# Attention stage of a streaming encoder step: logits of odd items issued behind the projection parts, softmax weights of the two narrow tiles scaled by VectorE

## The chip, the cores and the metric

One core of a Trainium2 chip runs the whole program. The time is device microseconds (us) of one execution, and the comparison is of medians over several executions of the two kernels.

## What is computed

One layer over 640 tokens (512 of a prompt, 8 samples with 16 new frames each), width 1024, in fp32. Every product of two large matrices is made of three matmuls over split operands (a high and a low half of each), so that fp32 accuracy is kept.

```python
x = x + 0.5 * swiglu(rmsnorm(x, ffn1_norm), ffn1_w_gate, ffn1_w_up, ffn1_w_down)
h = rmsnorm(x, mix_norm)
z = h @ w_in                        # gates, conv inputs, q, k, v, index queries and keys
...
conv_out = gb * conv                # 3-tap causal conv of gc * xv
score = einsum(relu(index dots), wi); top n_sel keys of each token
logits = einsum(q, k_sel) * HEAD_DIM ** -0.5
p = softmax(logits); o = einsum(p, v_sel)
x = x + concat([conv_out, attn]) @ w_out
x = x + 0.5 * swiglu(rmsnorm(x, ffn2_norm), ffn2_w_gate, ffn2_w_up, ffn2_w_down)
```

## The kernel before

The program has three stages: the first feed-forward block (to about 450 us), the mixer (450 to about 720 us) and the second feed-forward block. The change is nearly all in the last part of the mixer, the **attention items** (585 to 712 us).

**Items.** There are 40 items, `ITEMS[n]` for n = 0 to 39: five tiles of tokens in the order 3, samples, 2, 1, 0 (`ATT_TILES`, the samples are tile 4), and eight items (heads, or samples) in each. A tile's keys are 512, 384, 384, 256 and 128 columns wide. So items 16 to 23 are tile 2 (384 columns), items 24 to 31 tile 1 (256) and items 32 to 39 tile 0 (128); tiles 1 and 0 are the narrow ones. One item passes through these steps:

- TensorE writes the logits into PSUM bank 4 or 5 (`logits_pair`, two heads at once, L937; `logits_sample`, L921 to L926). It waits until the bank's last logits have been read.
- VectorE adds the mask, stores the sum into one of four weight slots and takes the row's minimum (`masked_min`, L2115, which frees the bank); for the samples it takes a minimum alone (L2109).
- ScalarE takes the exponential in place and its row sum (`exp_out`, L1418, or L1414 for the samples).
- The row is divided by its sum: on ScalarE for items 0 to 7, on VectorE for items 8 to 11 (`normalise`, L2126 and L2127), on GpSimd from item 12 (`GPSIMD_FROM`, L2353 and L2354).
- TensorE transposes the weights into bank 6 (`turn_weights`, L854), once per item in tiles 3, 4 and 2, once for two items in tile 1, once for four in tile 0. ScalarE copies the bank out (`weights_out`, L1102 `hid<-ps`), and TensorE multiplies by the values (`weigh_sample_values`, L965; `weigh_four_heads`, L979).

**Parts.** Between these, TensorE works off 64 *parts* (`filler`), each six matmuls of 320 columns (L596, L598, L600): 32 of the conv projection, then 32 of the output projection. `parts_by(n)` says how many are done by the end of item n; items 8, 12, 20, 28 and 36 have none. Parts left over follow item 39. When a block of parts is complete, VectorE evicts it (`proj_out`, L2077 for the output projection). Part 32 and its three followers need the conv output, split by ScalarE and VectorE (`conv_hi`, `conv_lo`, in items 8 to 11 by `CONV_SPLITS`).

**What sets the order.** It is written out by hand. Each engine runs its own loop over n. `issued_by(n)` gives how far the logits, the masked minima and the exponentials have been issued by item n: n + 3 up to item 14, 19 in item 15, n + 5 from item 16 on. A pair of logits is issued when its even item comes up, so from item 16 on in even items, behind `turn_weights` and ahead of the parts. VectorE's loop further holds the last rounds of the top-k selection (`top_rounds`, L2062 and L2063; the mask of tile 1 is finished in item 19, by `ROUNDS`), the low halves of the next weights in quarters (`quarter_lo_of`, L1557, by `QUARTERS`) or whole (`mixer_lo`, L1548), and the low half of a finished tile's output (`attended_lo`, L2134). ScalarE makes the high halves.

**In the feed-forward blocks** four hidden blocks are made in the plain way and the rest in pairs of sets inside a loop. `plain_hid(3)` (L1647, L1651), the last step of the fourth plain block, stands on VectorE behind the loop and ahead of the last pair (`period(PAIRS - 1, ...)`). Its result is first read by ScalarE's `rest_hi(1)`, behind the last pair.

## Time and profile before

| | before |
|---|---|
| median of three executions | 1164.75 us (1164.25 to 1165.76) |
| profiled execution, its time | 1166.49 us |
| profiled execution, its span | 1164.60 us |
| TensorE busy | 1154.6 us (99%) |
| VectorE busy | 916.1 us (79%) |
| ScalarE busy | 526.1 us (45%) |
| GpSimd busy | 94.7 us (8%) |

The span is what the profiler saw from the first to the last instruction, and 1.9 us lie around it. TensorE's busy share hides two things: matmuls run longer when a lower clock is granted and are still busy, and the page's slices of 29 us don't show waits of a few us. So the attention items have to be read in a timeline.

### The profile page before, as it was taken

What the parts mean: (1) busy time and instruction counts of PE and PEld (TensorE: products, weight loads), DVE (VectorE), ACT (ScalarE), POOL (GpSimd) and SP (SyncE); (2) the same over time, 40 slices, a digit from 0 to 9 for tenths busy, and PEclk for the clock granted to TensorE, in tenths of its full rate; (3) what the DMA queues carried; (4) which work ended last, traced back from release to release, by engine and by line L of the source; (5) the groups of instructions that cost most, each with busy time, mean ns of one, the idle gap of its engine ahead of it and who ended that gap; (6) DMA issues with size and microseconds to landing.
All of it is one profiled execution on the core that took longest, in us unless ns stands there. A gap on an engine that the chain in (4) does not pass through costs nothing.

```text
span 1164.6 us, 20299 instructions
## 1 busy us (share of the span) xinstructions
PE 1154.6 (99%) x7704; PEld 1107.3 (95%) x7704; DVE 916.1 (79%) x1402; ACT 526.1 (45%) x791; POOL 94.7 (8%) x130
## 2 busy tenths in 40 slices
PE   9999999999999999999999899999999999999999
PEld 9999999999999999867987679999999999999998
DVE  6998777877989982467998753798877778798996
ACT  6354444444445552361234452434444444454452
POOL 0000000000000000102473351000000000000000
PEclk9999999999999999999999899999999999999999
DMA  7212221222332233201321023321322222124222
GB/s 249 85 55 91 86 95 72 98 82 67 124 146 80 73 109 119 73 37 37 145 73 37 1 67 107 129 73 37 109 72 84 96 72 98 64 100 154 103 87 84
DMA packets 22992, 103.98 MB, mean 89 GB/s; under 512 B 3344, under 2 KB 6288, under 8 KB 13584
## 3 DMA queue, kind: packets, MB, share of 16 engines
q1 hardware_dynamic: 21792, 99.67, 24.2%
q10 hardware_dynamic: 1136, 3.43, 1.0%
q8 instruction: 43, 0.70, 0.3%
q14 instruction: 21, 0.17, 0.0%
HBM read 96.99 MB, written 6.10 MB: 89 GB/s over the span
## 4 chain that ended last, share of the span: by engine, by line
PE 91%; DVE 7%; issue 1%; ACT 1%; DVEq 0%; POOL 0%; ACTq 0%; POOLq 0%
PE ps L656 18%; PE ps L658 18%; PE ps L657 18%; PE ps L596 8%; PE ps L600 8%; PE ps L598 8%; PE ps L587 2%; PE ps L589 2%; PE ps L588 2%; DVE score L2063 1%; PE ps L854 1%; DVE top L2062 1%; DVE wl L1548 1%; PE ps L937 1%; PE ps L863 1%
## 5 line engine op out<-in xcount | busy, mean ns | idle before, releaser
L1102 ACT ACTIVATE wh<-raw 128x1024 fp32r<-128x1024 f32 (+4 forms) x206 | 202.4, 985 | 261.6 <-PE ps L658 142.9
L656 PE MATMUL ps<-xs,wh 128*128 128x320 f32 x976 | 300.2, 308 | 0.5 <-ACT snap L1102 0.5
L657 PE MATMUL ps<-xs,wh 128*128 128x320 f32 x976 | 300.2, 308 | 0.0
L658 PE MATMUL ps<-xs,wl 128*128 128x320 f32 x976 | 300.1, 308 | 0.0
L656 PEld LDWEIGHTS ps<-xs,wh 128*128 128x128 f32 x976 | 182.9, 187 | 1.0 <-issue 1.0
L658 PEld LDWEIGHTS ps<-xs,wl 128*128 128x128 f32 x976 | 182.9, 187 | 0.0
L657 PEld LDWEIGHTS ps<-xs,wh 128*128 128x128 f32 x976 | 182.9, 187 | 0.0
L596 PE MATMUL ps<-xh,wh 128*128 128x320 f32 x544 | 131.1, 322 | 0.0
L1672 DVE TENSOR_TENSOR wl<-raw,wh 128x1024 fp32r<-128x1024 f32 (+1 forms) x108 | 112.7, 1044 | 19.4 <-ACT wh L1102 18.3
L600 PE MATMUL ps<-xh,wl 128*128 128x320 f32 x544 | 124.7, 311 | 0.0
L598 PE MATMUL ps<-xl,wh 128*128 128x320 f32 x544 | 124.6, 311 | 0.0
L1102 ACT ACTIVATE snap<-ps 128x320 f32<-128x320 f32 x156 | 68.0, 437 | 121.1 <-PE ps L658 120.6
L596 PEld LDWEIGHTS ps<-xh,wh 128*128 128x128 f32 x544 | 90.0, 189 | 12.6 <-issue 11.1
L598 PEld LDWEIGHTS ps<-xl,wh 128*128 128x128 f32 x544 | 91.8, 189 | 0.0
L600 PEld LDWEIGHTS ps<-xh,wl 128*128 128x128 f32 x544 | 91.7, 189 | 0.0
L658 PE MATMUL ps<-xr,wl 128*128 128x320 f32 x288 | 88.9, 309 | 0.0
L656 PE MATMUL ps<-xr,wh 128*128 128x320 f32 x288 | 88.9, 309 | 0.0
L657 PE MATMUL ps<-xr,wh 128*128 128x320 f32 x288 | 88.9, 309 | 0.0
L1672 DVE TENSOR_TENSOR wl<-sums,wh 128x1024 fp32r<-128x1024 f32 x36 | 44.1, 1225 | 38.1 <-ACT wh L1102 38.1
L1102 ACT ACTIVATE wh<-sums 128x1024 fp32r<-128x1024 f32 x52 | 54.8, 1053 | 24.0 <-DVE sums L1687 14.4
L1548 DVE TENSOR_TENSOR wl<-raw,wh 128x2048 fp32r<-128x2048 f32 (+2 forms) x31 | 56.5, 1823 | 11.5 <-ACT wh L1102 11.5
L1783 DVE TENSOR_TENSOR wl<-raw,wh 128x1024 fp32r<-128x1024 f32 (+1 forms) x48 | 49.9, 1041 | 6.1 <-ACT wh L1102 6.1
(282 smaller groups left out, 2134.4 us busy)
## 6 DMA issues: line engine op xcount, KB each, us to landing
raw<-gu SPq DMA_DIRECT2D x42, 1024.0 KB, 4.8
raw<-dn SPq DMA_DIRECT2D x16, 1024.0 KB, 5.3
raw<-dn SPq DMA_DIRECT2D x12, 512.0 KB, 3.8
raw<-wconv SPq DMA_DIRECT2D x6, 1024.0 KB, 4.9
raw<-wout SPq DMA_DIRECT2D x4, 1024.0 KB, 4.8
x<-xt SPq DMA_DIRECT2D x12, 320.0 KB, 4.7
raw<-wtok SPq DMA_DIRECT2D x4, 840.0 KB, 4.3
x_keep<-x SPq DMA_DIRECT2D x8, 320.0 KB, 2.2
```

Source lines behind the costliest of these rows:

```text
L587: pe.matmul(out, ah, bh, start=first, stop=False)
L588: pe.matmul(out, ah, bl, start=False, stop=False)
L596: pe.matmul(o, ah, bh[:, c], start=first, stop=False)
L598: pe.matmul(o, ah, bl[:, c], start=False, stop=False)
L600: last_mm = pe.matmul(o, al, bh[:, c], start=False, stop=last)
L656: pe.matmul(out, ah, bh, start=first, stop=False, skip_group_check=True)
L657: pe.matmul(out, ah, bl, start=False, stop=False, skip_group_check=True)
L658: return pe.matmul(out, al, bh, start=False, stop=last, skip_group_check=True)
L1102: return nc.scalar.activation(out, in_, ACT.Copy, scale=scale)
L1548: dve.tensor_tensor(wl[:, slot, 0:n], raw[:, slot, 0:n], wh[:, slot, 0:n].bitcast(F32), ALU.subtract).then_inc(lo_ready, 1)
L1672: dve.tensor_tensor(ring(wl_flat, part), set_source(slot, part), ring(wh_flat, part).bitcast(F32), ALU.subtract)\
L1783: dve.tensor_tensor(ring(wl_flat, part), set_source(slot, part), ring(wh_flat, part).bitcast(F32), ALU.subtract)\
```

## The change

1. **Order of the logits.** `issued_by(n)` is n + 4 from item 15 on. The pairs of logits are then issued in odd items (18 and 19 in item 15, 20 and 21 in item 17, and so on), and behind the parts instead of ahead of them. On VectorE the masked minima from item 15 on stand at the end of an item, behind the top rounds, evictions and quarters; ScalarE's exponentials follow the same `issued_by`.
2. **Parts one item earlier.** Item 8 has a part, and four parts instead of five are left after item 39. `CONV_SPLITS` moves to items 7 to 10 and waits for `chunks_used` (the first four chunks of the last conv block have been read) instead of for all conv projections.
3. **The first unit of output weights in quarters.** The high and low halves of `U_OUT` are made in four quarters in items 4 to 7, not whole in item 3. The third unit's quarters move from items 27, 28, 29 and 33 to 26, 27, 28 and 32. In item 15 ScalarE makes its quarter ahead of the exponentials.
4. **Scaling of the narrow tiles.** Items 24 to 39 are divided by their sums on VectorE (`VECTOR_FROM` = 24), the weights of item n + 2 in item n, and no longer on GpSimd.
5. **Feed-forward blocks.** `plain_hid(3)` moves on VectorE into the last half period of the last pair, and ScalarE waits for it ahead of `rest_hi(1)`.

```diff
@@ parts_by, tables, issued_by @@
-            return 32 + n - 8 - sum(m <= n for m in WITHOUT_PART)
+            return 32 + n - 7 - sum(m <= n for m in WITHOUT_PART)
...
-        PROJ_SPLITS = {0: U_CONV + 5, item_of(9): U_OUT}
-        QUARTERS = {14 + q: (U_OUT + 1, q) for q in range(4)}
+        PROJ_SPLITS = {0: U_CONV + 5}
+        QUARTERS = {4 + q: (U_OUT, q) for q in range(4)}
+        QUARTERS |= {14 + q: (U_OUT + 1, q) for q in range(4)}
...
-        GPSIMD_FROM = 12
+        GPSIMD_FROM, VECTOR_FROM = 12, 24
...
-            return min(n + 3 if n < 15 else 19 if n == 15 else n + 5, len(ITEMS))
+            return min(n + 3 if n < 15 else n + 4, len(ITEMS))
...
-        CONV_SPLITS = {8: (0,), 9: (1,), 10: (2,), 11: (3,)}
+        CONV_SPLITS = {7: (0,), 8: (1,), 9: (2,), 10: (3,)}
@@ TensorE, loop over the items @@
-                for ahead in range(issued_by(n - 1), issued_by(n)):
-                    logits(ahead)
+                if n < 15:
+                    for ahead in range(issued_by(n - 1), issued_by(n)):
+                        logits(ahead)
                 for i in range(parts_by(n - 1), parts_by(n)):
                     filler(i)
+                if n >= 15:
+                    for ahead in range(issued_by(n - 1), issued_by(n)):
+                        logits(ahead)
@@ ScalarE @@
+                act.wait_ge(hid_ready, PLAIN * (k + 1))
                 for n in (1, 2):
                     rest_hi(n)
...
                 if n in CONV_SPLITS:
-                    act.wait_ge(proj_job, NPROJ)
+                    act.wait_ge(chunks_used, 1)
...
-                if n in QUARTERS and ITEMS[n][0] != 4:
+                if n in QUARTERS and (ITEMS[n][0] != 4 or n == 15):
                     quarter_hi_of(*QUARTERS[n])
@@ VectorE, feed-forward @@
+                    if not ahead:
+                        plain_hid(3)
                     out_of(p, slot, 0, block)
...
-                plain_hid(3)
                 period(PAIRS - 1, 0, pair_block(PAIRS - 1))
@@ VectorE, normalise and the loop over the items @@
-                wait_bank_read(dve, job)
+                if t == 4:
+                    wait_bank_read(dve, job)
+                else:
+                    dve.wait_ge(exp_ready, nth_of_kind(n) + 1)
...
+                if VECTOR_FROM <= n + 2 < len(ITEMS):
+                    normalise(n + 2)
+                if n < 15:
+                    for ahead in range(issued_by(n - 1), issued_by(n)):
+                        masked_min(ahead)
...
                 if n in (25, 33):
                     attended_lo(n // 8 - 1)
+                if n >= 15:
+                    for ahead in range(issued_by(n - 1), issued_by(n)):
+                        masked_min(ahead)
@@ GpSimd @@
-            for n in range(GPSIMD_FROM, len(ITEMS)):
+            for n in range(GPSIMD_FROM, VECTOR_FROM):
                 normalise(n)
```

TensorE in item 15 before, from its transposes to those of item 16 (`tab` holds the identity of the transposes, `kt,q_all` are logits, `xh`, `xl` with `wh`, `wl` a part, `hid` with `ikc_v`, `zkv` the product with the values):

```order
L854 MATMUL ps<-tab,score 128x128 x3
L937 MATMUL ps<-kt,q_all 128x384 x2
L596 MATMUL ps<-xh,wh 128x320 x2
L598 MATMUL ps<-xl,wh 128x320 x2
L600 MATMUL ps<-xh,wl 128x320 x2
L965 MATMUL ps<-hid,ikc_v 64x64 x2
L965 MATMUL ps<-hid,zkv 64x64
L965 MATMUL ps<-hid,ikc_v 64x64 x2
L965 MATMUL ps<-hid,zkv 64x64
L854 MATMUL ps<-tab,rp 128x128 x3
```

The same place after:

```order
L857 MATMUL ps<-tab,score 128x128 x3
L599 MATMUL ps<-xh,wh 128x320 x2
L601 MATMUL ps<-xl,wh 128x320 x2
L603 MATMUL ps<-xh,wl 128x320 x2
L942 MATMUL ps<-kt,q_all 128x384 x2
L973 MATMUL ps<-hid,ikc_v 64x64 x2
L973 MATMUL ps<-hid,zkv 64x64
L973 MATMUL ps<-hid,ikc_v 64x64 x2
L973 MATMUL ps<-hid,zkv 64x64
L857 MATMUL ps<-tab,rp 128x128 x3
```

The part now stands ahead of the logits of items 18 and 19, and item 16 (from the last row on) has no logits of its own.

VectorE before, from the masked minimum of item 16 (first row) to that of item 18 (last row). `MAX` and `MATCH_REPLACE` are a top round of tile 1, `wl<-raw,wh` is a quarter:

```order
L2115 ISA rp,stat<-ps,mask 128x384
L2115 ISA stat 128x1
L2062 MAX top<-score 128x8
L2063 MATCH_REPLACE score<-top,score 128x256
L1557 TENSOR_TENSOR wl<-raw,wh 128x512
L2115 ISA rp,stat<-ps,mask 128x384
L2115 ISA stat 128x1
L2115 ISA hid,stat<-ps,mask 128x384
```

The same place after:

```order
L2129 ISA rp,stat<-ps,mask 128x384
L2129 ISA stat 128x1
L2076 MAX top<-score 128x8
L2077 MATCH_REPLACE score<-top,score 128x256
L1570 TENSOR_TENSOR wl<-raw,wh 128x512
L2076 MAX top<-score 128x8
L2077 MATCH_REPLACE score<-top,score 128x256
L1570 TENSOR_TENSOR wl<-raw,wh 128x512
L2129 ISA rp,stat<-ps,mask 128x384
L2129 ISA stat 128x1
L2129 ISA hid,stat<-ps,mask 128x384
L2129 ISA stat 128x1
```

A second top round and a second quarter now stand ahead of the masked minimum of item 17.

VectorE in tile 1 before, from the masked minimum of item 26 on:

```order
L2115 ISA rp,stat<-ps,mask 128x256
L2115 ISA stat 128x1
L2077 SCALAR_TENSOR_TENSOR x<-ps,x 128x640
L2115 ISA rp,stat<-ps,mask 128x256
L2115 ISA stat 128x1
L2115 ISA hid,stat<-ps,mask 128x256
L2115 ISA stat 128x1
L2115 ISA hid,stat<-ps,mask 128x256
```

VectorE in tile 1 after, from the masked minimum of item 24 on:

```order
L2129 ISA rp,stat<-ps,mask 128x256
L2129 ISA stat 128x1
L2143 RECIPROCAL stat<-stat 128x1
L2144 TENSOR_SCALAR rp<-rp,stat 128x256
L2129 ISA rp,stat<-ps,mask 128x256
L2129 ISA stat 128x1
L2143 RECIPROCAL stat<-stat 128x1
L2144 TENSOR_SCALAR rp<-rp,stat 128x256
```

Each masked minimum is now followed by the reciprocal and the multiply of the same item, and only then by the next masked minimum.

## Rows read from the trace of the kernel before

**Rows 1.** waits of TensorE: us in total, times, longest

```profile
PE ps L937 <- DVE stat L2115: 4.0, 3, 2.4
...
PE ps L656 <- ACT snap L1102: 0.5, 2, 0.2
...
PE ps L965 <- ACT hid L1102: 0.4, 1, 0.4
...
PE ps L854 <- DVE rp L2127: 0.3, 1, 0.3
```

**Rows 2.** windows: length, busy PE, PEld, DVE, ACT, POOL, PEclk, DMA share, GB/s

```profile
640.00:657.00 17.00, 17.00 (x165) 12.26 (x160) 14.53 (x37) 7.71 (x20) 5.48 (x8) 1.00 0.00 1
...
660.00:680.00 20.00, 18.82 (x94) 13.30 (x94) 11.99 (x37) 10.10 (x26) 9.14 (x15) 0.68 0.25 83
```

**Rows 3.** timeline of PE: start, us, engine, line, operation, [idle before <-releaser]

```profile
656.97 0.55 PE L854 MATMUL ps<-tab,score 128*128 128x128 f32 x3
...
659.91 1.65 PE L937 MATMUL ps<-kt,q_all 64*128 64x384 f32 x4 [2.39 <-DVE stat L2115]
...
666.53 1.65 PE L937 MATMUL ps<-kt,q_all 64*128 64x384 f32 x4 [1.14 <-DVE stat L2115]
...
669.88 0.84 PE L854 MATMUL ps<-tab,rp 128*128 128x128 f32 x3
...
672.12 0.84 PE L854 MATMUL ps<-tab,hid 128*128 128x128 f32 x3
...
674.72 0.49 PE L854 MATMUL ps<-tab,score 128*128 128x128 f32 x3
...
676.02 1.51 PE L979 MATMUL ps<-hid,zkv 128*64 128x256 f32 x12
...
680.27 0.52 PE L854 MATMUL ps<-tab,hid 128*128 128x128 f32 x3 [0.18 <-ACT hid L1102]
...
705.53 0.60 PE L854 MATMUL ps<-tab,rp 128*128 128x128 f32 x4
```

**Rows 4.** timeline of DVE, 650 to 666 us

```profile
650.26 0.56 DVE L2109 TENSOR_REDUCE stat<-ps 128x1 f32<-128x384 f32 x1 [0.56 <-PE ps L926]
...
655.93 0.82 DVE L2077 SCALAR_TENSOR_TENSOR x<-ps,x 128x640 f32<-128x640 f32 x1
...
656.67 0.55 DVE L2115 CUSTOM_DVE_ANT_0 rp<-ps,mask 128x384 f32<-128x384 f32 x1
...
658.59 0.69 DVE L1557 TENSOR_TENSOR wl<-raw,wh 128x512 fp32r<-128x512 f32 x1 [0.51 <-ACT wh L1102]
...
659.20 0.55 DVE L2115 CUSTOM_DVE_ANT_0 rp<-ps,mask 128x384 f32<-128x384 f32 x1
...
665.23 0.69 DVE L2134 TENSOR_TENSOR xl<-ps,xh 128x512 fp32r<-128x512 f32 x1 [1.04 <-ACT xh L1102]
```

**Rows 5.** timeline of DVE and of ACT: one narrow item's operations

```profile
638.27 0.15 DVE L2126 RECIPROCAL stat<-stat 128x1 f32<-128x1 f32 x1
...
638.45 0.42 DVE L2127 TENSOR_SCALAR rp<-rp,stat 128x384 f32<-128x384 f32 x1
...
678.68 0.42 DVE L2115 CUSTOM_DVE_ANT_0 rp<-ps,mask 128x256 f32<-128x256 f32 x1 [1.54 <-PE ps L937]
...
678.05 0.49 ACT L1102 ACTIVATE hid<-ps 128x384 f32<-128x384 f32 x1 [1.36 <-PE ps L854]
...
679.15 0.51 ACT L1418 ACTIVATE rp<-rp,stat 128x256 f32<-128x256 f32 x1 [0.60 <-DVE stat L2115]
...
679.57 0.19 ACT L1418 ACTIVATION_READ_ACCUMULATOR rp<-rp,stat 128x1 f32 x1
...
698.76 0.40 ACT L1418 ACTIVATE rp<-rp,stat 128x128 f32<-128x128 f32 x1 [1.67 <-DVE stat L2115]
```

**Rows 6.** timeline, end of the first feed-forward loop: DVE, then PE

```profile
265.93 0.82 DVE L1647 SCALAR_TENSOR_TENSOR hid<-sq_pair,hid 128x640 f32<-128x640 f32 x1
...
270.86 0.39 PE L656 MATMUL ps<-xs,wh 128*128 128x320 f32 x1 [0.25 <-ACT snap L1102]
```

More of the change, by code:

```diff
@@ L230, in trunk @@
         proj_job = sem("proj_job")
+        chunks_used = sem("chunks_used")
         proj_evac = sem("proj_evac")
@@ L260, in trunk @@
         p_ready = sem("p_ready")
+        p_narrow_ready = sem("p_narrow_ready")
         p_sample_ready = sem("p_sample_ready")
@@ L350, in quarters_before @@
         def quarters_before(U):
-            return 3 * (0 if U == U_CONV else U - U_OUT)
+            return 3 * (0 if U == U_CONV else 1 + U - U_OUT)
         def first_part(buf, i):
@@ L894, in proj_part @@
                     pe.wait_ge(lo_ready, U + 1)
-                    if U in (U_CONV, U_OUT + 1, U_OUT + 2):
+                    if U in (U_CONV, U_OUT, U_OUT + 1, U_OUT + 2):
                         pe.wait_ge(quarter_lo, quarters_before(U) + 3)
@@ L909, in proj_part @@
                     mm.then_inc(proj_job, 1)
+                if b == NPROJ - 1 and c == 3:
+                    mm.then_inc(chunks_used, 1)
             def proj(b):
@@ L949, in turn_weights @@
             def turn_weights(n):
-                pe.wait_ge(p_sample_ready if ITEMS[n][0] == 4 else p_ready, nth_of_kind(n) + 1)
+                if n >= VECTOR_FROM:
+                    pe.wait_ge(p_narrow_ready, n - VECTOR_FROM + 1)
+                else:
+                    pe.wait_ge(p_sample_ready if ITEMS[n][0] == 4 else p_ready, nth_of_kind(n) + 1)
                 first = n if n < 24 else n - 1 if n < 32 else n - 3
@@ L1525, in _ @@
                     exp_out(ahead)
-                if n in QUARTERS and ITEMS[n][0] == 4:
+                if n in QUARTERS and ITEMS[n][0] == 4 and n != 15:
                     quarter_hi_of(*QUARTERS[n])
@@ L2124, in normalise @@
                 job = ("logit", n)
-                wait_bank_read(dve, job)
+                if t == 4:
+                    wait_bank_read(dve, job)
+                else:
+                    dve.wait_ge(exp_ready, nth_of_kind(n) + 1)
                 link(dve.reciprocal(stat[:, 80 + n:81 + n], stat[:, 40 + n:41 + n]))
                 dve.tensor_scalar(weights(n)[:, 0:width[t]], weights(n)[:, 0:width[t]], stat[:, 80 + n:81 + n],
-                                  None, ALU.mult).then_inc(p_sample_ready, 1)
+                                  None, ALU.mult).then_inc(p_sample_ready if t == 4 else p_narrow_ready, 1)
             def attended_lo(i):
@@ L2250, in _ @@
                     normalise(n + 1)
-                for ahead in range(issued_by(n - 1), issued_by(n)):
-                    masked_min(ahead)
+                if VECTOR_FROM <= n + 2 < len(ITEMS):
[3 more added lines that the diff above has]
+                        masked_min(ahead)
                 for t, rounds in ROUNDS.items():
```

## The prediction

> **What bounds the kernel now.** I read the list of TensorE's waits first, then the windows over the attention items, then TensorE's timeline there and VectorE's beside it. TensorE is the bound: it is busy 99% of the span, so work on other engines counts only where it makes TensorE wait, or where it keeps TensorE at its lower clock. The list shows about 7 us of waits in all; 4.0 of them are logits that wait for VectorE's masked minimum [rows 1]. Two of the three lie in items 15 and 16: 2.39 us ahead of the logits of items 18 and 19, and 1.14 us ahead of those of 20 and 21 [rows 3]. What the list doesn't show is the clock. In the window from 660 to 680 us the mean granted clock is 0.68, in that from 640 to 657 us it is 1.00 [rows 2]. 0.68 means 12.8 us at 1.2 GHz and the rest at 2.4 GHz, and the fall comes with the 2.39 us wait. At the low clock, transposes and a part take 2.24 us (669.88 to 672.12), at the full one 1.30 (674.72 to 676.02) [rows 3], a factor of about 1.75. Of the 12.8 us, 1.1 are waiting, so 11.7 x (1 - 1/1.75) = 5.0 us are lost to the clock. The attention items thus lose 2.39 + 1.14 + 5.0 = 8.5 us around items 15 to 18, and 0.8 elsewhere (0.4, 0.3 and 0.18 [rows 1, 3]). Everything behind 720 us is TensorE without a wait, so what the items gain or lose passes to the end.
>
> The wait of 2.39 us is VectorE running behind. It last waits for TensorE at 650.26 us (samples' logits of item 14) and then has no pause up to the masked minimum of item 16 at 656.67; that of item 17 follows at 659.20 and releases TensorE 0.71 us later [rows 3, 4].
>
> **Feed-forward part of the change.** `plain_hid(3)` takes 1.6 us on VectorE just ahead of the last pair, and TensorE waits 0.25 us for a snapshot there [rows 6]; the list has it twice, 0.5 us in all, once per block [rows 1]. In its new place VectorE has no set to sum for a next pair, which is what hides it. The new wait on ScalarE holds `rest_hi(1)`, and behind it the operands of the rest units, until a step that was done some 10 us before. I take the 0.5 us as gained; if the cover were missing, 1.6 us on VectorE would come back as at most 0.5 us here. **-0.5 us.**
>
> **Items 0 to 14.** The first unit's halves are made in quarters in items where TensorE doesn't wait, instead of whole; the sum of the work is the same. The transfer that follows into the freed buffer starts four items later and is needed only from item 26. Parts come one item earlier: item 8 has one, and it hides the two waits of items 8 and 9 (0.4 and 0.3 us, for ScalarE's copy and VectorE's scaling [rows 1]). A part is 1.0 of the 1.30 us that transposes and a part take [rows 3]; this one is saved behind item 39, where parts follow each other and take 0.9. `chunks_used` lets the conv halves start before the last projection is complete. If a half came late instead, item 8's part would wait, by something like those 0.7 us. So item 15 starts at 656.97 + 1.0 - 0.7 = 657.3 us [rows 3].
>
> **Items 15 to 21.** Here the new order is decided. VectorE's waiting point of item 12 shifts with TensorE by 0.3 to 650.6; the masked minimum of item 16 came 6.41 us behind it, of which 0.74 are an eviction (655.93 to 656.67) that now lies in item 11 [rows 4]: 656.3. Before, the minimum of item 17 followed 2.53 us behind (a top round, a quarter, 0.5 us of waiting for ScalarE). Now one more top round (658.59 - 656.67, less 0.51 of waiting and 0.47 for the minimum = 0.94) and one more quarter (658.59 to 659.20 = 0.61) stand ahead of it: 656.3 + 2.53 + 0.94 + 0.61 = 660.4, and TensorE is released 0.71 later, at 661.1 [rows 4]. TensorE has its transposes and the part behind it at 657.3 + 1.3 = 658.6 to 658.7. **The part no longer comes behind the wait but ahead of it, and the wait is as long as it was, 2.4 us**, since VectorE's share in front of it grew by 1.55 us.
>
> The clock will then most likely fall again. The first stretch without any wait brought it back before (from 669.88 [rows 3]), and now TensorE has work from 661.1 for 5 to 7 us (logits, product, and the parts of items 16 and 17). I take 3 us of loss; the ends are 0 and some 6.
>
> The next pair (20, 21) waits for the minimum of item 19. Its row of VectorE work: the minimum of 18 at 662.7 (logits at the low clock take 1.65 us [rows 3]), `attended_lo` (with 1.0 us of waiting for ScalarE before it, as at 665.23 [rows 4]), a top round, an eviction, a quarter, the minimum: 668.1. TensorE is there at about 667.8, waits some 0.4 us, and issues at 668.3. Then the minimum of item 20 (0.94 + 0.61 + 0.55 after 668.1) and its exponential hold ScalarE's copy of the transposes of item 18, and item 19's transposes start at 671.4, 1.0 us late. Item 19 is 1.3 us for transposes and part, 0.85 for logits and 1.45 for the product with the values [rows 3], so item 20 starts at 675.0. Now the transposes of 20 and 21 stand back to back, where a pair of logits lay between; the second needs the bank copied out (0.55 [rows 3] + 0.49 [rows 5] and 0.1 of signals = 1.15 instead of 0.5). With 2.0 us for item 21, **item 22 starts at 678.0** against 680.27 before, and one part more is done by then. At full clock all through it would be 677.2, with a long low stretch 679.5.
>
> **Items 22 to 39.** GpSimd's 16 scalings hid behind everything; on VectorE they form a chain. VectorE's queue is now minimum n, reciprocal and multiply n, minimum n + 1, and the multiply needs the exponential of the same item. The rows for 256 columns [rows 5]: 0.47 from the minimum to the exponential (678.68 to 679.15), 0.61 until the row sum is read, 0.03, 0.18 from reciprocal to multiply, and 0.27 for the multiply (0.33 of step at 384 columns, taken down for the width): 1.56 us. For 128 columns the same steps are 0.34 + 0.50 (0.40 and the sum's read-out [rows 5]) + 0.03 + 0.18 + 0.20 = 1.25, an estimate where no row has the width. That is 8 x 1.56 + 8 x 1.25 = 22.5 us, in which nothing else fits, because the queue is in order. To it come four quarters (2.5), three evictions (2.2) and two `attended_lo` (0.6 of 0.69 each): 28.4 us [rows 4]. The chain starts 0.2 us behind item 22's start, waits about 1.3 us for TensorE (logits 26, eviction 15) and 0.6 for ScalarE's quarters and signals. So the transposes that end it, item 39's, start 30.7 us behind item 22. Before, they came 705.53 - 680.27 = 25.3 us behind [rows 3]. **+5.4 us**, in waits of 0.5 to 1.5 us ahead of the logits of 30, 32, 34, 38 and the product of 27 and 31. The low end, without the two additions, is 28.9 (+3.6); the high end 32.
>
> GpSimd, which loses this work, has nobody waiting for it: `norm_factors(2)`, behind it in its queue, comes later. Scaling would cost nothing if the cover were still there; it is the order of the queue that costs.
>
> **The sum,** by marks of the timeline: item 39's transposes at 678.0 + 30.7 = 708.7 against 705.5 (+3.2); one part less behind them (-0.9); the feed-forward waits (-0.5). That is **+1.8 us**: a span of 1166.4 us, 1168.3 for a profiled execution with the 1.9 us around it. The median shown is 1.7 us under the profiled execution before, so the median comes to 1164.75 + 1.8 = **1166.5 us**.
>
> **Rivals.** (a) *The clock falls again in the narrow tiles* or stays low for longer than I take in items 15 to 19. For it: the chain leaves TensorE idle in short pieces, and two (1.2 us each) are 4 us apart in items 27 to 29. Against it: 0.6 us of waits at 637 to 639 us brought no fall. The price is 1 to 4 us on the forecast, 1168 to 1170.5, since TensorE has slack to the chain for part of it. The Trainium skill (TensorE: Matmul & The Clock Gate, "A second HAM failure mode: psum-queue depth-cycling") tells of a kernel whose clock swung because TensorE was idle for moments between groups of matmuls. By that page this rival would be the rule; no row here shows such a fall. It decides if the median is above 1168. (b) *The chain doesn't bind.* If exponentials are ready before VectorE comes to the multiply, the narrow tiles keep their 25.3 us: 1166.5 - 5.4 = 1161.1. It would take VectorE two minima ahead, and the queue shows that it can't be. (c) *No second fall* at item 15, since the transposes are now followed by a part: item 22 at 677.2 and the chain at its low end, 0.8 + 1.8 us better: 1164. (d) *The reordering does nothing*: waits only change places, 1164.75.
>
> **Chances.** The forecast (1165.5 to 1168) 0.42, (a) 0.24, (b) or anything beyond 2.3 us of gain 0.14, (c) and (d) 0.20. A change of 0.2% (2.3 us) is about what a measurement of this kernel can tell from none. The forecast itself lies within it, and a quarter of it and most of (a) beyond: faster 0.15, same 0.48, slower 0.37. Range 1162.8 to 1170.0.
>
> **What would show it.** Right: a wait of about 2.4 us ahead of the logits of items 18 and 19, behind a part; a granted clock below 1 around 660 us, for less than 12.8 us; item 22's transposes near 678; VectorE in tile 1 with a wait for ScalarE ahead of each reciprocal, 1.5 us from minimum to minimum, and TensorE waits summing to 4 to 6 us between items 22 and 39; no snapshot wait at 271 us. Wrong: no wait at item 15 (then my VectorE count from 650 us is off), or TensorE without waits in the narrow tiles (then the chain is hidden).

## The result and the profile after

The changed kernel takes 1169.63 us (median of six executions, 1169.39 to 1171.06), the kernel before 1165.2 us in the same session (1164.25 to 1166.27). The ratio is 1.0044, 95% interval 1.0033 to 1.0055: by the medians 4.4 us **slower**. The profiled execution took 1171.06 us with a span of 1169.1 us, 4.5 us over the span before.

TensorE's waits after (us in total, times, longest):

```profile
PE ps L942 <- DVE stat L2129: 7.5, 7, 2.3
PE ps L857 <- ACT hid L1114: 2.9, 4, 1.7
PE ps L987 <- ACT hid L1114: 1.4, 3, 0.5
...
PE ps L857 <- DVE rp L2144: 0.8, 1, 0.8
```

The waits for the masked minimum (L2129; the logits are at L942) grew from 4.0 us in three to 7.5 us in seven [rows 1]. Waits for ScalarE's copies of the transposed weights (`hid`) come to 4.3 us, where they were 0.6. The two waits for a snapshot [rows 1] are gone. The timeline of TensorE at the marks of [rows 3], which are the transposes of items 15, 19, 22 and 39 and the logits of (18, 19) and (20, 21):

```profile
658.79 0.55 PE L857 MATMUL ps<-tab,score 128*128 128x128 f32 x3
...
662.51 1.65 PE L942 MATMUL ps<-kt,q_all 64*128 64x384 f32 x4 [2.30 <-DVE stat L2129]
...
669.59 0.92 PE L942 MATMUL ps<-kt,q_all 64*128 64x384 f32 x4 [1.41 <-DVE stat L2129]
...
673.78 0.52 PE L857 MATMUL ps<-tab,score 128*128 128x128 f32 x3 [1.67 <-ACT hid L1114]
...
680.59 0.55 PE L857 MATMUL ps<-tab,hid 128*128 128x128 f32 x3
...
711.42 0.66 PE L857 MATMUL ps<-tab,rp 128*128 128x128 f32 x4
```

Item 15 starts 1.8 us later than before (one part more is done by then), item 22 0.3 later, item 39 5.9 later. The span is 4.5 us longer, so behind item 39 the changed kernel is 1.4 us faster. Two windows, with the granted clock in the third column from the right:

```profile
656.00:664.00 8.00, 5.70 (x38) 3.52 (x36) 5.66 (x17) 3.32 (x8) 3.65 (x6) 0.91 0.00 0
...
690.00:712.00 22.00, 17.28 (x121) 13.68 (x120) 13.28 (x55) 10.87 (x33) 0.00 (x0) 1.00 0.13 49
```

The clock falls again at the wait of 2.30 us, and for less time: the mean from 660 to 680 us is 0.91, where it was 0.68 [rows 2]. By the same working as in the prediction that is 3.6 us at 1.2 GHz and 1.5 us lost, 3.5 less than before. In the narrow tiles TensorE is idle for 4.7 of 22 us, in short pieces, and the clock stays at 2.4 GHz. The balance of the two profiles: all waits of TensorE sum to 15.0 us instead of 7.2, 7.8 more, and 3.5 us less are lost to the clock; that makes 4.3 of the 4.5 us.

### The profile page after: what moved, and what is told of

It is laid out like the page before. It is cut to its first block, busy times and chain, and to the rows that moved or that the text cites. A ratio compares the mean times of both kernels' runs of the same rounds, so it can differ in the third digit from the quotient of the medians.

```text
span 1169.1 us, 20306 instructions
## 1 busy us (share of the span) xinstructions
PE 1151.4 (98%) x7704; PEld 1104.6 (94%) x7704; DVE 925.8 (79%) x1437; ACT 526.1 (45%) x794; POOL 78.7 (7%) x98
## 4 chain that ended last, share of the span: by engine, by line
PE 86%; DVE 10%; issue 2%; ACT 2%; DMA 1%; ACTq 0%; DVEq 0%
PE ps L659 18%; PE ps L660 18%; PE ps L661 18%; PE ps L599 7%; PE ps L603 7%; PE ps L601 7%; PE ps L590 2%; PE ps L592 2%; PE ps L591 2%; DVE score L2077 2%; DVE top L2076 2%; DVE wl L1561 1%; PE ps L866 1%; PE ps L857 1%; DMA raw<-gu 1%
```

## The experiments

Each kernel was timed beside the kernel before. In the table, "15 to 22" is the time from the transposes of item 15 to those of item 22 in the profiled execution, "22 to 39" the same for the items behind; both are differences of two starts in TensorE's timeline, as above. The kernel before has medians of 1164.10 to 1165.2 us in the different sessions, so kernels of two sessions are compared here by what each is above or below the kernel before. A star marks a stretch in which that execution had a low clock for some microseconds.

| kernel | median us | before, same session | ratio (95%) | 15 to 22 | 22 to 39 |
|---|---|---|---|---|---|
| before | 1165.2 | | | 23.30* | 25.26 |
| after | 1169.63 | 1165.2 | 1.0044 (1.0033 to 1.0055) | 21.80* | 30.83 |
| e1 after, scaling on GpSimd | 1169.15 | 1164.57 | 1.0041 (1.0028 to 1.0055) | 22.87* | 29.76 |
| e2 after, scaling behind the minimum | 1168.36 | 1164.57 | 1.0040 (1.0026 to 1.0054) | 21.51* | 29.66 |
| e3 before, scaling on VectorE | 1164.89 | 1164.57 | 1.0004 (0.9995 to 1.0013) | 19.83 | 25.92 |
| e4 before, part 5 | 1163.42 | 1164.57 | 0.9990 (0.9981 to 0.9999) | 19.84 | 25.25 |
| e5 before, part 1 | 1168.84 | 1164.10 | 1.0035 (1.0021 to 1.0048) | 21.15* | 29.12 |
| e6 e1, minimum of 17 earlier | 1168.10 | 1164.10 | 1.0031 (1.0021 to 1.0042) | 19.94 | 29.76 |
| e7 after, minimum of 17 earlier | 1169.17 | 1164.10 | 1.0035 (1.0022 to 1.0049) | 20.89* | 30.82 |
| e8 before, parts 2 and 3 | 1163.28 | 1164.10 | 0.9990 (0.9981 to 0.9999) | 20.66* | 25.44 |
| e9 e1, quarters behind the minimum | 1164.30 | 1164.22 | 1.0002 (0.9993 to 1.0012) | 18.87 | 27.68 |
| e10 after, quarters behind the minimum | 1164.61 | 1164.22 | 1.0003 (0.9994 to 1.0012) | 18.88 | 28.07 |
| e11 after, quarters and scaling behind it | 1163.84 | 1164.22 | 0.9997 (0.9988 to 1.0006) | 18.87 | 27.49 |
| e12 before, parts 2, 3, 5, minimum of 17 in item 14 | 1160.36 | 1164.22 | 0.9967 (0.9954 to 0.9979) | 17.41 | 25.45 |
| e13 e11, logits ahead of the parts | 1169.81 | 1164.16 | 1.0053 (1.0039 to 1.0066) | 21.69* | 30.47 |
| e14 before, minimum of 17 in item 14 | 1161.42 | 1164.16 | 0.9976 (0.9967 to 0.9985) | 18.21 | 25.26 |
| e15 before, parts 2, 3, 5 | 1162.66 | 1164.16 | 0.9984 (0.9975 to 0.9993) | 19.89* | 25.43 |
| e16 e12, scaling of item 9 first | 1160.19 | 1164.16 | 0.9966 (0.9954 to 0.9978) | 17.67* | 25.43 |

### Is it the scaling? (e1 to e3)

The forecast had put 5.4 us on the scaling of the narrow tiles, so that was undone first.

```diff
-        GPSIMD_FROM, VECTOR_FROM = 12, 24
+        GPSIMD_FROM, VECTOR_FROM = 12, 40
```

> The changed kernel with part 4 alone undone: all weights from item 12 on are divided on GpSimd again. Theory A (the scaling on VectorE costs the time): items 22 to 39 took 25.3 us before and 30.8 after, so about 5.5 us go: 1164.1 us, 1.1 us faster than before, TensorE waits of about 5 us in items 22 to 39 gone. Rival B (the logits behind the parts are what costs there, whoever scales): less than 2 us go, 1168 us or more. Rival C (half each): 1166 to 1167.

Theory A fell: the kernel is still 4.6 us above the kernel before, where the changed one is 4.4, and items 22 to 39 still take 29.76 us. In them 1.1 us came back, not 5.5. Rival B had the number right. VectorE's timeline shows why. After, from the masked minimum of item 28 (first row) to that of item 30:

```profile
689.64 0.41 DVE L2129 CUSTOM_DVE_ANT_0 hid<-ps,mask 128x256 f32<-128x256 f32 x1
689.98 0.08 DVE L2129 DVE_READ_ACCUMULATOR2_ANT stat<- 128x1 f32 x1
690.73 0.16 DVE L2143 RECIPROCAL stat<-stat 128x1 f32<-128x1 f32 x1 [0.67 <-ACT hid L1431]
690.93 0.35 DVE L2144 TENSOR_SCALAR hid<-hid,stat 128x256 f32<-128x256 f32 x1
691.25 0.69 DVE L1570 TENSOR_TENSOR wl<-raw,wh 128x512 fp32r<-128x512 f32 x1
691.86 0.42 DVE L2129 CUSTOM_DVE_ANT_0 hid<-ps,mask 128x256 f32<-128x256 f32 x1
...
693.96 0.69 DVE L1570 TENSOR_TENSOR wl<-raw,wh 128x512 fp32r<-128x512 f32 x1 [0.45 <-ACT wh L1114]
694.56 0.42 DVE L2129 CUSTOM_DVE_ANT_0 score<-ps,mask 128x256 f32<-128x256 f32 x1
```

The same place in e1, VectorE and then ScalarE:

```profile
689.24 0.41 DVE L2129 CUSTOM_DVE_ANT_0 hid<-ps,mask 128x256 f32<-128x256 f32 x1
...
690.85 0.69 DVE L1570 TENSOR_TENSOR wl<-raw,wh 128x512 fp32r<-128x512 f32 x1 [1.19 <-ACT wh L1114]
691.46 0.42 DVE L2129 CUSTOM_DVE_ANT_0 hid<-ps,mask 128x256 f32<-128x256 f32 x1
...
693.56 0.71 DVE L1570 TENSOR_TENSOR wl<-raw,wh 128x512 fp32r<-128x512 f32 x1 [1.67 <-ACT wh L1114]
694.19 0.41 DVE L2129 CUSTOM_DVE_ANT_0 score<-ps,mask 128x256 f32<-128x256 f32 x1
```

```profile
689.70 0.51 ACT L1431 ACTIVATE hid<-hid,stat 128x256 f32<-128x256 f32 x1 [1.59 <-DVE stat L2129]
690.12 0.18 ACT L1431 ACTIVATION_READ_ACCUMULATOR hid<-hid,stat 128x1 f32 x1
690.21 0.61 ACT L1114 ACTIVATE wh<-raw 128x512 fp32r<-128x512 f32 x1
691.92 0.51 ACT L1431 ACTIVATE hid<-hid,stat 128x256 f32<-128x256 f32 x1 [1.10 <-DVE stat L2129]
```

With and without the scaling it is 2.22 us from the first minimum to the second, and 2.70 or 2.73 to the third. In e1 VectorE stands for 1.19 and 1.67 us ahead of each quarter (`wl<-raw,wh`), for ScalarE's quarter (`wh<-raw`); that one stands in ScalarE's queue behind the exponential, the exponential waits for the minimum, and the next minimum stands on VectorE behind the quarter. That is a **second loop between the two queues**: minimum 0.46 us, exponential with its sum 0.5, ScalarE's quarter 0.6, VectorE's quarter 0.6. In the changed kernel the scaling lies in VectorE's waits within that loop, and one turn of 2.22 us is one item. The kernel before has the same chain, but with the minimum of item n + 4 at the start of item n, ahead of that item's quarter, a turn leads to the next minimum but one. So it spans two items, which take 3.0 us of TensorE's time on average (25.26 us for 17 items), and the turn does not hold them up.

> The changed kernel with one line moved: on VectorE the scaling of item n + 2 stands behind the masked minimum of item n + 3 instead of ahead of it. The same operations on the same engine. Theory A1 (the cost is the serial chain minimum, exponential, reciprocal, multiply of one item, 1.56 us at 256 columns): VectorE no longer stands for 0.67 us ahead of each reciprocal, items 22 to 39 take 26 us or less, 1164.5 to 1165.5 us. Rival A2 (the cost is VectorE's load, 16 x 0.6 us more, in whatever order): 3 us or more of the 5.5 stay, 1167.5 us or more.

The edit moves `normalise(n + 2)` behind `masked_min(n + 3)`. Theory A1 fell: VectorE no longer waits ahead of each reciprocal, and items 22 to 39 take 29.66 us all the same. Rival A2 had the number (1168.36 us), but not the cause, as e3 and e11 show. The median is 0.8 us lower than e1's in the same session; the ratios, 1.0040 and 1.0041, don't tell the two apart. The loop through the quarters is untouched: 2.22 and 2.71 us from minimum to minimum at the same place.

> The kernel before with part 4 alone: items 24 to 39 divided on VectorE, item n + 2 in item n. There the masked minimum of item n + 3 already stands between the minimum and the scaling of item n + 2. Theory A1 (chain): the chain never forms, within 0.7 us of before, 1165 to 1166 us. Rival A2 (load): 3 to 5.5 us slower, 1168 to 1171 us.

```diff
+                if VECTOR_FROM <= n + 2 < len(ITEMS):
+                    normalise(n + 2)
                 for ahead in range(issued_by(n - 1), issued_by(n)):
                     masked_min(ahead)
```

The cut shows the line that matters; the semaphore and the limits of the two loops are as in the diff of the change. Part 4 alone, in the order before, costs nothing that can be measured (1.0004), and 0.66 us in the profile's items 22 to 39. VectorE's load is not the cause.

### Which part loses the time (e4, e5, e8)

> The kernel before with part 5 alone: plain_hid(3) inside the last half period of the last pair. Theory: the two snapshot waits of 0.25 us go, 0.5 us faster, 1164.7 us. Rival (its 1.6 us on VectorE come back at the end of the pair or in the rest units): 1165.2 us or more.

The edit is the two places of `plain_hid(3)` in the diff of the change. Part 5 alone gives 1.1 us by the medians, at the edge of what can be told from nothing (0.1 to 2.2 us by the interval), where 0.5 was expected. The two snapshot waits are gone from its trace, and the timelines show some more: TensorE is 0.74 us behind the kernel before at 25 us and 0.31 behind it at 416 us, a gain of 0.43 in the first block, and behind item 39's transposes the span is 458.63 us instead of 459.07, 0.44 in the second. That is 0.9 us for waits that the list gives as 0.5; the rest of each is not explained.

> The kernel before with part 1 alone: logits pairs in odd items behind the parts, masked minima from item 15 on at the end of an item, and ScalarE's quarter of item 15 ahead of its exponentials (without which that order locks up). The scaling stays on GpSimd. Theory B (the place of the masked minima costs: a second chain through the quarters, minimum, exponential, ScalarE's quarter, VectorE's quarter, minimum, 2.2 us for each item with a quarter): nearly all of the change's loss is here, 1168 to 1170 us, items 22 to 39 in 29 to 30 us. Rival A (the scaling is the cause, and its undoing was hidden by something else): within 1.5 us of before, 1164.5 to 1166.5 us.

```diff
-            return min(n + 3 if n < 15 else 19 if n == 15 else n + 5, len(ITEMS))
+            return min(n + 3 if n < 15 else n + 4, len(ITEMS))
@@ VectorE @@
-                for ahead in range(issued_by(n - 1), issued_by(n)):
-                    masked_min(ahead)
+                if n < 15:
+                    for ahead in range(issued_by(n - 1), issued_by(n)):
+                        masked_min(ahead)
...
+                if n >= 15:
+                    for ahead in range(issued_by(n - 1), issued_by(n)):
+                        masked_min(ahead)
```

The cut leaves out TensorE's logits behind the parts and ScalarE's quarter of item 15, which are as in the diff of the change. Part 1 alone is 4.7 us slower by the medians: the whole loss. Items 22 to 39 take 29.12 us with all the scaling on GpSimd. Theory B holds.

> The kernel before with parts 2 and 3 alone: parts one item earlier, the conv halves in items 7 to 10, the first unit of output weights in quarters in items 4 to 7. Theory: a part more stands ahead of item 9, the two waits of items 8 and 9 (0.61 us) go but 0.8 us return ahead of item 9's transposes, and one part less follows item 39: about 0.3 us slower, 1164.8 to 1165.5 us. Rival (the quarters and the slow conv halves cost nothing by themselves, the 0.8 us come with the rest of the change): 0.6 us faster, 1164 us.

The edit is all of the diff on parts, tables, `CONV_SPLITS` and `chunks_used`. Parts 2 and 3 alone are 0.8 us **faster**, against my expectation and near the rival's 0.6, although the wait of 0.80 us ahead of item 9 is there (639.96 in its timeline). TensorE then comes later to the wait ahead of the logits of 18 and 19, which shrinks from 2.39 to 1.59 us.

### Taking the loops apart (e6, e7, e9 to e11)

> The changed kernel with the scaling on GpSimd again and, on VectorE, from item 15 on the masked minimum of item n + 2 at the start of item n, ahead of top rounds, evictions, attended_lo and quarters (TensorE's order stays that of the change). Theory B: both chains are gone; no wait ahead of the logits of 18 and 19, items 22 to 39 in 25 to 26 us: 1160 to 1163 us, faster than before. Rival D (TensorE's own order, logits behind the parts and transposes back to back, is what costs): 1165 us or more. If the clock at 660 us stays full without that wait, the wait is what brings the fall; if it falls all the same, it is not.

```diff
+                if n >= 15 and n + 2 < len(ITEMS):
+                    masked_min(n + 2)
                 if n == 16 or n == 8:
                     attended_lo(n // 8 - 1)
...
-                if n >= 15:
-                    for ahead in range(issued_by(n - 1), issued_by(n)):
-                        masked_min(ahead)
```

Theory B's number fell, and rival D's (1165 us or more) came out. But the expectation rested on a misreading of my own edit. The start of item n + 1 is the same place in the queue as the end of item n, so only the minimum of item 17 really moved; the loop through the quarters stayed (29.76 us, as in e1). What the run does show: the wait ahead of the logits of 18 and 19 fell from 2.31 to 0.72 us, and 0.73 us ahead of item 17 and 0.79 more ahead of the next pair took nearly all of it back.

> As the kernel with the minima first and GpSimd's scaling, but with the scaling on VectorE as in the change, so that the minimum of item n + 2 and the scaling of item n + 2 stand side by side: the chain of the scaling alone, without the one through the quarters. Theory (two chains of nearly the same length, each of which holds the time alone): items 22 to 39 take 29.5 to 31 us again, 4 to 5 us more than with GpSimd, 1165 to 1167 us. Rival (the scaling never cost anything, in any order): within 1 us of the kernel with GpSimd.

The same edit on the changed kernel, with the same misreading in it: the loop through the quarters is still there, so this is no test of the scaling's chain alone. Items 22 to 39 take 1.1 us more than in e6, and in after 1.1 us more than in e1. So the scaling adds 1.1 us there to a loop that is there already. The medians are 1.1 us apart, too, but the intervals of e6 and e7 overlap nearly whole.

> The changed kernel with the scaling on GpSimd and, on VectorE from item 15 on, the quarter of an item behind its masked minimum instead of ahead of it. Neither chain is left. Theory (two chains, either of which holds items 22 to 39 at 29 to 31 us; the trace of the kernel with the scaling back on GpSimd shows 2.2 to 2.7 us from minimum to minimum wherever a quarter stands between): items 22 to 39 in 25.3 to 26.5 us, 1163.5 to 1165.5 us. Rival D (TensorE's order itself: logits behind the part, transposes back to back): items 22 to 39 stay above 28 us, 1167 us or more.

```diff
-                if n in QUARTERS:
+                if n in QUARTERS and n < 15:
                     quarter_lo_of(*QUARTERS[n])
                 if n in (25, 33):
                     attended_lo(n // 8 - 1)
                 if n >= 15:
                     for ahead in range(issued_by(n - 1), issued_by(n)):
                         masked_min(ahead)
+                if n in QUARTERS and n >= 15:
+                    quarter_lo_of(*QUARTERS[n])
```

With the quarter moved behind the minimum, and nothing else against e1, the time falls from 4.6 us above the kernel before to 0.1 above it, 4.5 us. VectorE's timeline of e9 at the place shown for e1:

```profile
685.48 0.41 DVE L2129 CUSTOM_DVE_ANT_0 hid<-ps,mask 128x256 f32<-128x256 f32 x1
...
685.82 0.42 DVE L2129 CUSTOM_DVE_ANT_0 hid<-ps,mask 128x256 f32<-128x256 f32 x1
...
687.09 0.69 DVE L1570 TENSOR_TENSOR wl<-raw,wh 128x512 fp32r<-128x512 f32 x1 [0.84 <-ACT wh L1114]
687.79 0.42 DVE L2129 CUSTOM_DVE_ANT_0 score<-ps,mask 128x256 f32<-128x256 f32 x1
```

The second minimum now follows 0.34 us behind the first instead of 2.22, the third 2.31 behind the first instead of 4.95. Items 15 to 22 also gain (18.87 us): there, too, a quarter stood ahead of each minimum. The 22.87 us of e1 hold a low clock; e6, with the quarter still ahead and the full clock, takes 19.94. All eleven executions of e9 have a mean clock of 1.000, those of e1 0.997 to 1.000, so a part of the 4.5 us is the clock. Items 22 to 39 take 27.68 us, 2.1 less than in e1 but 2.4 more than before; my 25.3 to 26.5 was too low.

> The changed kernel with only the quarters moved behind the minima; the scaling stays on VectorE ahead of the minimum. The chain of the scaling alone. Theory: items 22 to 39 in 29.5 to 31 us, 3.5 to 5 us more than in the same kernel with GpSimd's scaling, 1167 to 1169.5 us. Rival (the scaling is hidden once the quarters are out of the way): within 1 us of that kernel.

The scaling chain alone costs 0.4 us in items 22 to 39 and 0.3 us in the medians against e9: the theory of two loops of the same length fell. The scaling's chain is there, with 1.55 to 1.60 us from minimum to minimum in items 28 to 31, but TensorE takes 1.5 us for an item anyway, so it holds up little. The trace of e10 shows the quarters filling the chain's gaps; no wait stands ahead of this reciprocal, where after has 0.67 us:

```profile
687.88 0.69 DVE L1570 TENSOR_TENSOR wl<-raw,wh 128x512 fp32r<-128x512 f32 x1
688.63 0.16 DVE L2143 RECIPROCAL stat<-stat 128x1 f32<-128x1 f32 x1
688.83 0.35 DVE L2144 TENSOR_SCALAR hid<-hid,stat 128x256 f32<-128x256 f32 x1
```

> The changed kernel with quarters and scaling both behind the minimum: on VectorE minimum of n + 3, scaling of n + 2, quarter. No chain, all the scaling still on VectorE. Theory: as with GpSimd's scaling to within 0.7 us, 1163.5 to 1166 us. Rival A2 (VectorE's load of 16 x 0.6 us counts in any order): 2 us or more above the kernel with GpSimd's scaling and quarters behind.

As expected: 1163.84 us with all the scaling on VectorE, within 0.5 us of e9. Two moved lines in VectorE's loop take the changed kernel back to the median of the kernel before. They don't undo all that part 1 costs: parts 2, 3 and 5 without it are 1.5 us faster than before (e15), this kernel 0.4, and its items 22 to 39 take 27.49 us instead of 25.26.

### What else TensorE's order does (e13)

> The changed kernel with quarters and scaling behind the minimum on VectorE, and on TensorE the pairs of logits of odd items ahead of the parts again instead of behind them. That kernel without the last edit took 27.5 us for items 22 to 39, 2.2 us more than before, in short waits for ScalarE's copies of the transposes. Theory (the 2.2 us come from the place behind the parts): items 22 to 39 in 25.5 to 26.5 us, 1 to 2 us faster, 1162 to 1163 us. Rival (they come from issuing pairs in odd items at all, where ScalarE's copy of the last transposes is not covered): within 0.5 us of 1163.8 us, or slower by what TensorE then waits for the minimum, up to 1166 us.

```diff
-                if n < 15:
-                    for ahead in range(issued_by(n - 1), issued_by(n)):
-                        logits(ahead)
+                for ahead in range(issued_by(n - 1), issued_by(n)):
+                    logits(ahead)
                 for i in range(parts_by(n - 1), parts_by(n)):
                     filler(i)
-                if n >= 15:
-                    for ahead in range(issued_by(n - 1), issued_by(n)):
-                        logits(ahead)
```

Both expectations failed by far: it is 6.0 us slower than e11. TensorE's waits in e13:

```profile
PE ps L942 <- DVE stat L2125: 7.0, 6, 2.6
PE ps L857 <- DVE rp L2140: 2.2, 2, 1.4
PE ps L857 <- ACT hid L1110: 1.8, 2, 1.1
```

The logits then wait for a minimum that comes at an item's end, and the part that could have run meanwhile stands behind them. So the placing behind the parts is worth some 6 us *given* minima at the end of an item; it is the right half of part 1. The 2.2 us that items 22 to 39 of e11 take more than before stay open: in its trace they are waits of 0.36 to 0.62 us for ScalarE's copies and for the scaling, but no run took their cause away.

### The minimum of item 17 (e12, e14 to e16)

```diff
-                for ahead in range(issued_by(n - 1), issued_by(n)):
+                for ahead in (16, 17) if n == 14 else (18,) if n == 15 else range(issued_by(n - 1), issued_by(n)):
                     masked_min(ahead)
```

> The kernel before with one step moved: VectorE's masked minimum of item 17 right behind that of item 16. It tells what of the 3.9 us comes from this step. Theory: the wait of 2.4 us ahead of logits 18 and 19 goes, 1 to 1.5 us of it come back one pair later, and the clock has no fall in any execution, which the kernel before shows in a part of its executions (up to 2 us in its median): 1161.5 to 1163 us. Rival (VectorE bounds the stretch as a whole, the waits only move): 1163.5 to 1164.5 us.

One step moved in the kernel before gives 2.7 us by the medians, 0.1 us beyond the theory's band. TensorE's timeline shows the wait of 2.39 us [rows 3] at 0.34, and the next one at 2.06 instead of 1.63 (e3's, with the same clock):

```profile
657.88 0.92 PE L937 MATMUL ps<-kt,q_all 64*128 64x384 f32 x4 [0.34 <-DVE stat L2115]
...
663.07 0.92 PE L937 MATMUL ps<-kt,q_all 64*128 64x384 f32 x4 [2.06 <-DVE stat L2115]
```

Against e3 and e4, which have the order before and the full clock, items 15 to 22 take 18.21 us instead of 19.83, so 1.6 us are waits. The rest of the gain is, as far as the clocks tell, the clock: the mean granted clock was 1.000 in ten of eleven executions and 0.999 in the other, and the times lie between 1160.78 and 1162.38 us. For the kernel before in the same session they lie between 1163.31 and 1166.35 us at 0.994 to 0.999.

> The kernel before with parts 2, 3 and 5, without the moved minimum. Theory (0.8 and 1.1 us add up): 1162 to 1162.8 us. Rival (one of the two was only the spread of the executions): 1163.2 us or more.

1.5 us faster, within the theory's band; the gains of e4 and e8 add up to 2.0.

> The kernel before with parts 2, 3 and 5 and one step more: VectorE makes the masked minimum of item 17 right behind that of item 16, in item 14, ahead of the top rounds and the quarter of items 14 and 15. Parts 2 and 3 gave 0.8 us and part 5 gave 1.1 us alone. Theory: the wait ahead of the logits of 18 and 19 falls from 2.4 us to under 1 us, a part of it comes back ahead of the logits of 20 and 21: 1160.5 to 1162.5 us, and the clock stays full there in all executions. Rival (what the wait loses comes back in full one pair later, since VectorE is what bounds items 12 to 19): 1162.5 to 1163 us.

1160.36 us, 3.9 us faster than before: a version that beats both kernels. 1.1 us of it come on top of e14, 2.4 on top of e15. It is 0.1 us below the theory's band. There is no wait left ahead of the logits of 18 and 19; 1.67 us stand ahead of the next pair and 1.18 ahead of the one behind it.

> The kernel of 1160.4 us with VectorE's scaling of item 9 ahead of the conv half of item 8, which takes 1.58 us there instead of 0.83. Theory: TensorE's wait of 0.80 us ahead of item 9's transposes goes; but what TensorE gains there it waits again at the next masked minimum that it needs, since VectorE's work up to that one is the same: within 0.4 us of 1160.4 us. Rival (the wait is lost time): 0.6 to 0.8 us faster, 1159.6 us.

```diff
+                if n == 8:
+                    normalise(n + 1)
                 for i in CONV_SPLITS.get(n, ()):
                     conv_lo(i)
-                if 8 <= n + 1 < GPSIMD_FROM:
+                if 8 <= n + 1 < GPSIMD_FROM and n != 8:
                     normalise(n + 1)
```

1160.19 us, the same. The wait of 0.80 us is gone from the trace, but 0.20 and 0.34 us stand ahead of item 9's product and item 10's transposes. GpSimd's conv step now lies beside the scaling, which takes 0.93 us instead of 0.42. Item 22's transposes start 39.7 us behind item 8's in both kernels: 0.3 us are gained up to item 15 and gone by item 22, where e16's profile has a low clock (0.57 from 664 to 668 us) and e12's has not. So most of the wait at item 9 came back at once, not at a later minimum, as I had written.

## Why the prediction was wrong, point by point

The forecast was no change that can be measured, 1166.5 us; it is 4.4 us slower. The range held it by 0.4 us, the sign was not the likeliest one. The step that failed is that of items 22 to 39: it put +5.4 us on the scaling of the narrow tiles. The runs show +4.7 us for the new order alone (e5) and nothing that can be measured for the scaling alone (e3). The number was too low for another reason, smaller terms ahead of item 22. In us, what each stretch adds, by the marks of the two profiles, rounded:

| | forecast | measured |
|---|---|---|
| start of the program | 0 | 0.8 |
| `plain_hid(3)`, both blocks | -0.5 | -0.9 |
| items 0 to 14, one part more | +0.3 | +1.4 |
| items 15 to 21 | -2.6 | -1.5 |
| items 22 to 39 | +5.4 | +5.6 |
| one part less behind item 39 | -0.9 | -0.9 |
| sum | +1.8 | +4.5 |

- **The start of the program.** Not in the sum: 0.8 us. TensorE's sums of squares (`ps<-ones,sq_pair`), which stood at 24.52 us, stand at 25.33. The profile after has waits of 0.20 us at 9.83 and 25.33 us that the profile before has not; e4's has them too, e3's has not. No edit of e4 lies ahead of them. It is spread between executions.
- **The feed-forward blocks, -0.5 us.** The mechanism held, the size was too small. Of the 0.81 us, 0.39 are left at 416 us, so the first block gained 0.42; behind item 39 the second gained some 0.5. e4 shows the same two gains by itself.
- **Items 0 to 14, item 15 at 657.3 us.** Measured 658.79, 1.5 us later; 0.4 us of that are the start less the first feed-forward block. The other 1.1 us are the step that a part hides the two waits of 0.4 and 0.3 us: it does, but a new one of 0.80 us stands ahead of item 9's transposes. The conv half of item 8 takes 1.58 us on VectorE where it took 0.88:

```profile
637.61 1.87 POOL L2362 TENSOR_TENSOR conv_o<-conv_o,sq_pair 128x640 f32<-128x640 f32 x1 [1.70 <-DVE sq_pair L2108]
```

```profile
638.58 1.58 DVE L2113 TENSOR_TENSOR xl<-conv_o,xh 128x640 fp32r<-128x640 f32 x1
```

GpSimd's row ends at 639.48, and from there to the end of VectorE's are 0.68 us. The step one item earlier runs into GpSimd's last conv step. The Trainium skill (SBUF — State Buffer, "SBUF: two separate sides") says that a VectorE instruction with two inputs from SBUF and a GpSimd instruction that reads it share a port pair as an exclusive lock; these two rows agree. I had moved the conv halves in the sum without looking at what GpSimd does there. e8 is faster with it, and without that wait e16 has the same median as e12, so no run shows that it cost time in the end.
- **Items 15 to 21, 20.7 us.** Measured 21.80. The mechanism held: the part comes ahead of the wait, the wait is 2.30 us (forecast 2.4), the clock falls for a shorter time. The stretch became 1.5 us shorter, not 2.6. The mis-sized terms are the wait ahead of the logits of 20 and 21, 1.41 us (forecast 0.4), and the one ahead of item 19, 1.67 us (forecast 1.0); the clock took back part of it, 1.5 us lost instead of 3. And the gain itself is only one against a profile with 5.0 us lost to the clock: e3 and e4, in the order before and at the full clock, take 19.83 us for this stretch, 2.0 less than after.
- **Items 22 to 39, 30.7 us.** Measured 30.83: the number came out, **and its cause did not**. This is the step that a reader should keep. I added up VectorE's queue, found scaling, quarters, evictions and minima in one chain, and put the 5.4 us on what the change had added to it, the scaling. The links were right: 1.57 and 1.25 us from one item's scaling to the next in the trace after, where nothing else lies between. But the same queue without the scaling takes 29.76 us (e1), and with part 1 as the only change 29.12 (e5). Of the 5.6 us, 1.1 go with the scaling (e1), 2.1 with the quarter ahead of the minimum (e9), and 2.4 stay with the rest of part 1, without a run that takes them apart. "Scaling would cost nothing if the cover were still there; it is the order of the queue that costs" was the true half of it. The terms add up to 30.5 us, not 30.7. The sum should have been made twice, once with each part alone.
- **Behind item 39, -1.4 us.** Measured 5.89 - 4.5 = 1.4. That is partly luck: the forecast counts both feed-forward blocks there, and the first lies ahead of item 39.
- **The rivals.** (a), the clock falling in the narrow tiles, is refuted by the window from 690 to 712 us above: clock 1.00 with 4.7 us of idle time in it. The swings of the clock that the Trainium skill (TensorE: Matmul & The Clock Gate, "A second HAM failure mode: psum-queue depth-cycling") tells of do not show in this window. Its other half, a clock low for longer in items 15 to 19, is refuted as well, 1.5 us lost instead of 3. The time came out where (a) put it, for another reason. (b), the chain doesn't bind, was dismissed because VectorE would have to be ahead. It need not be: in e10 it still waits ahead of reciprocals, and the chain costs 0.4 us, since a link is hardly longer than an item of TensorE. (c), no second fall, does not give the time either: two of the six executions have a mean clock of 1.000, and they took 1169.45 and 1169.48 us. (d), the waits only change places, is what e6 and e16 show for single steps, not for the change.
- **The basis.** The profiled execution before was one with a clock of 0.994. The 5.0 us that its low clock costs are not in every execution: the profiles of e3 and e4 have the same wait of 2.38 and 2.39 us and no fall. Nor are they 5.0 us of the time. Without the fall, 1.6 us more of waits stand in items 15 to 21 (1.63 instead of 1.14, and new ones of 0.16 and 1.00), and item 22 comes 3.5 us sooner behind item 15 (19.83 instead of 23.30). The 21 executions of the kernel before in the session of e1 to e4 lie between 1163.2 and 1166.55 us, the ones at 0.994 above 1166.2. The chance of a fall belongs in the forecast, not one fall.

My estimates were 0.8 us (start), 1.1 (items 0 to 14), 1.1 (items 15 to 21) and 0.1 us (items 22 to 39) too low, and 0.4 us (feed-forward) too high: 2.7 us, the difference between +1.8 and +4.5.

## What to carry to other kernels

Two in-order queues that feed each other make a loop wherever A's step n + 1 stands behind something that B makes behind A's step n; look for it by following one step around both queues, and give one of the steps an item's lead. It costs where a turn is longer than the items of the bounding engine that it spans (2.22 us against 1.5 us here, and against 3.0 with the lead). When a chain is found, price each part of the change alone against it: what was added to the chain may lie in waits that another edit made. And a wait that shrinks is gained only if the next one on the same supplier does not grow; the same minimum made earlier gave 2.7 us in the order before (e14) and 0.6 in that of the change (e6, 4.0 us above the kernel before instead of e1's 4.6).

## What the runs showed of the hardware

The same instructions with the same wait fall to the low clock in some executions and not in others. The kernel before, e3 and e4 are the same in the attention items up to item 21. Windows of e3 over the stretch where the profile before has 0.68 [rows 2]:

```profile
656.00:664.00 8.00, 4.92 (x45) 3.42 (x43) 5.82 (x17) 4.62 (x12) 4.17 (x7) 1.00 0.00 0
664.00:672.00 8.00, 6.72 (x41) 5.15 (x41) 6.76 (x20) 4.28 (x11) 3.59 (x7) 1.00 0.00 0
```

TensorE waited 2.38 and then 1.63 us there, more than the 1.14 of the second wait before, at the full clock throughout. In e7 it waited only 0.72, 0.73 and 1.74 us, and the clock fell; e6 has the same three waits and the full clock. Windows of e7, then of e6:

```profile
664.00:672.00 8.00, 6.15 (x25) 4.47 (x25) 6.90 (x21) 3.53 (x10) 2.33 (x5) 0.63 0.21 61
```

```profile
664.00:672.00 8.00, 4.25 (x27) 3.23 (x28) 6.95 (x20) 3.50 (x9) 2.46 (x5) 1.00 0.12 35
```

In e5 it waited 3.09 us, up to 662.14, and the clock fell within 2 us behind the wait's end (0.97 from 660 to 664 us, 0.60 from 664 to 668). The length of a wait alone does not tell here whether the clock falls. The kernels with the minimum of item 17 in item 14 spread less than the kernel before: 1.6 us from lowest to highest in e14, 0.9 in e12 and 0.8 in e16, against 3.0. That step is not what it takes: e8, e9 and e15, without it, spread by 1.5, 1.6 and 1.7 us.
